# Two-layer NSA/MoBA decoder with experts: gathers and gate transposes moved in the expert pairs, half of layer 1's output projection in three fp32r products

## What is computed

```python
def reference(x, ...):
    for layer in range(2):
        mix = nsa_mixer(x, ...) if layer == 0 else moba_mixer(x, moba_w_in, moba_w_out)
        x = layer_norm(DN_ALPHA * x + mix, ...)
        x = layer_norm(DN_ALPHA * x + grouped_moe(x, ...), ...)
    return x

def moba_mixer(h, w_in, w_out):        # 256 tokens are one block: causal attention, 16 heads of 64
    q, k, v = split(h @ w_in, 3)       # w_in 1024 x 3072, rotary on q and k
    o = softmax(causal(q k^T / 8)) v
    return o @ w_out                   # the output projection, 1024 x 1024

def grouped_moe(h, router_w, router_bias, w_gate, w_up, w_down):   # 16 experts, 2 chosen per token
    gate = ...                         # 256 x 16, two nonzero in a row
    for e in range(16):
        he = silu(h @ w_gate[e]) * (h @ w_up[e])       # 1024 x 512 each
        out = out + (he @ w_down[e]) * gate[:, e:e+1]  # 512 x 1024
```

## Time and profile before

| | us |
|---|---|
| median of three runs | 739.78 (739.68 to 740.61) |
| the profiled execution, its own time | 741.22 |
| its span, from first to last instruction | 739.4 |
| expert matmuls begin, layer 0 / layer 1 | 172 / 522 |
| PE busy in the span | 721.2 (98%) |

### The profile page before, as it was taken

One profiled execution on the slowest core, in us unless ns is written; L12 is line 12 of the kernel. 1 busy time (PEld: TensorE's weight loads), 2 busy tenths in 40 slices (PEclk: granted clock), 3 DMA queues, 4 the chain that ended last, 5 costly groups with the idle time before them and its releaser, 6 DMA issues.

```text
span 739.4 us, 9052 instructions
## 1 busy us (share of the span) xinstructions
PE 721.2 (98%) x3696; PEld 391.8 (53%) x3696; DVE 281.5 (38%) x528; ACT 204.0 (28%) x467; POOL 110.1 (15%) x91
## 2 busy tenths in 40 slices
PE   9999999999999999999999999999999999999994
PEld 5877766774344344343368886646434434434331
DVE  4485675363212121121257785526322212112114
ACT  4443689332101110110033555714111011011001
POOL 0011378322000000000052221401200000000001
PEclk9999999999999999999999999999999999999998
DMA  9999900167999999999999964017799999999992
GB/s 329 304 368 418 405 3 1 58 233 297 423 425 429 430 425 429 426 425 422 413 388 387 414 267 187 6 57 285 271 425 428 425 428 428 428 425 429 419 412 84
DMA packets 45596, 245.06 MB, mean 331 GB/s; under 512 B 6256, under 2 KB 10480, under 8 KB 31728
## 3 DMA queue, kind: packets, MB, share of 16 engines
q1 hardware_dynamic: 45552, 244.43, 82.0%
HBM read 243.37 MB, written 1.05 MB: 331 GB/s over the span
## 4 chain that ended last, share of the span: by engine, by line
PE 88%; DVE 6%; ACT 2%; POOL 1%; issue 1%; DMA 1%; SPq 0%; DVEq 0%; ACTq 0%
PE ps L963 30%; PE ps L986 15%; PE ps L883 5%; PE ps L996 4%; PE ps L630 4%; PE ps L632 3%; PE ps L631 3%; PE ps L948 3%; PE ps L776 2%; PE ps L762 2%; PE ps L801 2%; ACT R L1273 1%; PE ps L974 1%; PE ps L939 1%; DVE R L1591 1%
## 5 line engine op out<-in xcount | busy, mean ns | idle before, releaser
L963 PE MATMUL ps<-ring,R 128*64 128x512 f32 x928 | 226.7, 595 | 0.0
L963 PEld LDWEIGHTS ps<-ring,R 128*64 128x64 f32 x928 | 70.3, 137 | 108.8 <-issue 107.2
L986 PE MATMUL ps<-ring,R 128*64 128x512 f32 x448 | 113.4, 595 | 0.8 <-issue 0.8
L1224 ACT ACTIVATE wh<-ps,small 128x512 fp32r<-128x512 f32 x32 | 22.0, 687 | 262.3 <-PE ps L986 260.5
L986 PEld LDWEIGHTS ps<-ring,R 128*64 128x64 f32 x448 | 35.8, 137 | 67.1 <-issue 64.8
L1578 DVE TENSOR_TENSOR wl_r<-ring,wh 128x512 fp32r<-128x512 f32 x72 | 55.4, 787 | 39.7 <-ACT wh L1202 39.3
L1804 DVE SCALAR_TENSOR_TENSOR wl_r<-ps,small,wh 128x512 fp32r<-128x512 f32 x32 | 24.0, 751 | 105.5 <-ACT wh L1224 104.7
L630 PE MATMUL ps<-wh,xh_r 128*128 128x512 f32 x144 | 57.7, 400 | 1.1 <-DVE wl_r L1578 1.0
L1202 ACT CAST wh<-ring 128x512 fp32r<-128x512 f32 x72 | 44.5, 623 | 47.3 <-PE ps L632 45.3
L632 PE MATMUL ps<-wh,xl 128*128 128x512 f32 x144 | 56.3, 391 | 0.0
L631 PE MATMUL ps<-wl_r,xh_r 128*128 128x512 f32 x144 | 56.1, 390 | 0.0
(11 more groups left out here) (237 smaller groups left out, 998.4 us busy)
## 6 DMA issues: line engine op xcount, KB each, us to landing
ring<-in_w_gate SPq DMA_DIRECT2D x24, 2048.0 KB, 17.5
ring<-in_w_up SPq DMA_DIRECT2D x18, 2048.0 KB, 18.7
ring<-in_w_down SPq DMA_DIRECT2D x18, 2048.0 KB, 19.2
ring<-in_w_in SPq DMA_DIRECT2D x20, 1024.0 KB, 14.4
ring<-in_w_gate SPq DMA_DIRECT2D x16, 1024.0 KB, 15.5
ring<-in_w_down SPq DMA_DIRECT2D x24, 512.0 KB, 20.1
ring<-in_w_up SPq DMA_DIRECT2D x12, 1024.0 KB, 11.5
ring<-in_w_out SPq DMA_DIRECT2D x8, 1024.0 KB, 14.9
```

The source lines that it names most:

```text
L963: last = mm(ps[64 * e:64 * e + 64, to, :], xe[:, j, at + 64 * e:at + 64 * e + 64], slots[e][:, j * UNIT:(j + 1) * UNIT], start=(j == 0), s ...
L986: last = mm(ps[64 * e:64 * e + 64, 2 + w, :], hT[:, k, 64 * e:64 * e + 64], slots[e][:, at:at + UNIT], start=(k == 0), stop=(k == FJ - 1))
```

## The change

1. In the expert pairs that gather (0 to 5): the transposes of the gate values move from between gate and up to behind the transposes of the hidden rows, and the second gather moves ahead of down and into bank 0. DVE's `slot_tables` and ACT's copy of gathered rows move accordingly.
2. Half a chunk of each expert phase, the first half of chunk 11 (`ROOM`), goes to a free place in R5, `room`, and is loaded right behind chunk 8.
3. In layer 1 the first four of eight blocks of the output projection become three fp32r products. ACT rounds the eight weight blocks (two units, four blocks) inside its loop over units 8 to 12, behind block 4 and block 7 of each (`out_weights_hi`), into the slot of unit 7; POOL subtracts behind the rotary adds. The attention output's first two groups are rounded by ACT (`group_hi`, behind the exponentials of items 5 and 7) and their rest is made by DVE in `collect`.
4. Unit 7's slot is busy longer, so the slots turn by one: only five chunks are loaded ahead of the end of layer 1's output projection, and chunk 7 comes in two halves.

```diff
-        PIECED = 6
+        PIECED = [6, 4]
...
+                if what == ("moe", 6 * PAIRS):
+                    line.append(line.pop(0))
...
+        ROOM = SLOT + 3
+        room = R5[:, 0:2 * D]
...
-            elif n in U0:
-                l = U0.index(n)
-                eng.wait_ge(L.proj, base[l].proj + T)
+            elif n == U0[0]:
+                eng.wait_ge(L.proj, base[0].proj + T)
+            elif n == U0[1]:
+                eng.wait_ge(L.mix, base[1].mix + 2 * T)
...
+            def load_first_of_split():
+                sp.wait_ge(L.mix, base[1].mix + T + 1)
+                load_part_of_split(0)
...
+            def load_room(n):
+                l = n // (6 * PAIRS)
+                sp.wait_ge(N.x_ready, ready(2 * l, T - 1, 1))
+                i, k = divmod(n % (6 * PAIRS), 6)
+                sp.dma_start(room, expert_src(l, 2 * i + k % 2, k // 2)[:, 0:2 * D]).then_inc(landing(("moe", n), 0)[0], 16)
...
-                ahead = SLOT - 2
+                ahead = SLOT - 2 - l
...
-                        if w and i % 2 and more:
-                            pe.wait_ge(rd.xa, 2 * g + 3)
+                        if i % 2 and more:
+                            pe.wait_ge((rd.xa, rd.xe)[w], 2 * g + 3)
+                        elif i and i % 2 == 0 and w == 0:
+                            pe.wait_ge(rd.xa, 2 * g + 2)
...
-                        if w == 0:
-                            pe.wait_ge(rd.gp, g + 1)
-                            if i:
-                                pe.wait_ge(rd.y_lo, 2 * n)
-                            transpose_gates(rd, 2 * (i % 2))
+                        if w == 0 and not more:
+                            gates_of_pair()
...
                     transpose_hidden(rd)
+                    if more:
+                        gates_of_pair()
...
                     pe.wait_ge(rd.ht_sb, n + 1)
+                    if more:
+                        gather(rd, 0, (2 * part + 2, 2 * part + 3), 4 * SLOTS)
                     pe.wait_ge(rd.gsum, n + 1)
...
-                    if more:
-                        pe.wait_ge(rd.xe, 2 * g + 2 + i % 2 + 1)
-                        gather(rd, 1, (2 * part + 2, 2 * part + 3), 4 * SLOTS)
...
+                def group_hi(u):
+                    act.wait_ge(L.pv, B.pv + ITEMS[l] // 4 * (u + 1))
+                    copy(OT2_HI[u], ps[:, 6 + u % 2, :]).then_inc(L.ot_sb, 1)
+
+                def out_weights_hi(n):
+                    w, j = WO[1][n]
+                    if n == 0:
+                        act.wait_ge(L.proj, base[1].proj + T)
+                    act.wait_ge(*landing(("unit", OUT[2 + w]), j // 4))
+                    copy(wo_hi_at(1, w, j), in_slot(("unit", OUT[2 + w]))[:, j * UNIT:(j + 1) * UNIT]).then_inc(wo_hi, 1)
...
                             split_hi(7 + i, j)
+                            if i < 5 and j in (4, 7):
+                                out_weights_hi(2 * (i - 1) + j // 7)
...
                     exponentials(m)
+                    if l and m in (5, 7):
+                        group_hi(m // 2 - 2)
...
+                    if l and r:
+                        out_weights_lo(r - 1, *WO[1][r - 1])
+                    if l and r == 7:
+                        out_weights_lo(7, *WO[1][7])
...
-                if l == 0 and u < 3:
+                if u < PIECED[l] // 2:
                     dve.wait_ge(L.ot_sb, B.ot_sb + 2 * u + 1)
                     tt(OT2_LO[u], ps[:, bank, :], OT2_HI[u], ALU.subtract).then_inc(L.ot_sb, 1)
```

More of the change, by code:

```diff
@@ L1 @@
 from collections import namedtuple
+from functools import partial
 from contextlib import ExitStack
@@ L314, in in_slot, with chunks_at @@
             return ring[:, n] if n < SLOT else extra
+        ROOM = SLOT + 3
+        room = R5[:, 0:2 * D]
+        def chunks_at(what, j):
+            if what[0] == "moe" and what[1] % (6 * PAIRS) == ROOM and j < KJ // 2:
+                return room[:, j * UNIT:(j + 1) * UNIT]
+            return in_slot(what)[:, j * UNIT:(j + 1) * UNIT]
+        spare_slots = [lambda j, n=n: ring[:, n, j * UNIT:(j + 1) * UNIT] for n in range(6)]
         def landing(what, h):
@@ L475, in load_half_freed @@
                             slot_free(what)
+                        if h == 0 and what[1] % (6 * PAIRS) == ROOM:
+                            continue
                         i, k = divmod(what[1] % (6 * PAIRS), 6)
@@ L557, in _ @@
                 for n in range(ahead, SLOT + 1):
+                    if ("moe", 6 * PAIRS * l + n) == SPLIT_FREED:
+                        load_rest_of_split()
+                        continue
                     load_expert(6 * PAIRS * l + n)
+                    if n == ahead and l:
+                        load_first_of_split()
+                load_room(6 * PAIRS * l + ROOM)
                 load_quarters(6 * PAIRS * l + SLOT + 1)
@@ L1008, in experts, with gates_of_pair @@
                     chunks = [("moe", 6 * n + k) for k in range(6)]
[L1009 removed]
+                    slots = [partial(chunks_at, c) for c in chunks]
                     more = i // 2 + 1 < DUOS
                     part = 2 * (i % 2)
+                    def gates_of_pair():
+                        pe.wait_ge(rd.gp, g + 1)
+                        if i:
+                            pe.wait_ge(rd.y_lo, 2 * n)
+                        transpose_gates(rd, 2 * (i % 2))
                     for w, done in ((0, rd.gate_done), (1, rd.up_done)):
@@ L1237, in experts @@
                     silu(rd)
+                    if i // 2 + 1 < DUOS:
+                        part = 2 * (i % 2) + 1
+                        act.wait_ge(rd.gathered, 4 * g + 4 + part + 1)
+                        copy_rows(rd, XeT[(i // 2 + 1) % 2], 0, range(2 * part, 2 * part + 2), 4 * SLOTS)
                     act.wait_ge(rd.gsum, n + 1)
@@ L1820, in experts @@
                         most = dve.value_load(over[0:1, 0:1], min_val=0, max_val=S)
-                    dve.wait_ge(rd.gt, n + 1)
-                    slot_tables(rd, i % 2)
+                    if not more:
+                        dve.wait_ge(rd.gt, n + 1)
+                        slot_tables(rd, i % 2)
                     dve.wait_ge(rd.silu, n + 1)
```

65 lines of the change are left out of this document (37 added, 28 removed).

## The result

The changed kernel took **766.78 us** (760.85 to 766.95, three runs) where the kernel before took 739.78: a ratio of 1.033, 95% interval 1.029 to 1.036. The profiled execution took 766.78, its span is 764.9 instead of 739.4. So it is slower, as forecast, but by 27 us and not by 11; 766.8 lies outside the range of 744 to 756.

What follows compares the result with a forecast made beforehand. PE's own sequence bounds the expert pairs, DMA close behind. Terms +7.1 +2.1 +1.2 +5.7 -2.2 -3.1 = +10.8 on the median 739.8 gave 750.6 us, range 744 to 756 (8 in 10).

Steps and rivals of the forecast that it cites:

- half clock behind one wait: Unit 8: after PE's idle time the clock stays at the lower level for a stretch, costing 2.1 us (0 to 3.4).
- Part 1: Expert pairs: the new order saves 0.51 us per gathering pair (0.35 to 0.65), 3.1 us per layer.
- Everything behind lands 2.5 us earlier, so 1.0 us of room is left: Expert pairs' DMA: the half chunk fills a hole, later chunks land 2.5 us earlier, and the gain stands in full.
- Part 2, the landing: Unit 8: ACT's cast waits for unit 13's first half, landing at 407.6; PE starts block 5 7.1 us later.
- the rival in which the weights do not hold ACT up: Unit 13's half there in time, keeping layer 0's gain: 738.3 us; needs landing 9 us earlier than 407.6; chance 0.05.
- the stretch 733 to 734: Profile row cited for the clock falling when PE rests: PE idle, granted 0.82, on its way from 1.00 to half.
- Part 2, contention: Layer 1's projection units: POOL's eight subtractions slow DVE at eight more meetings, most hidden: 1.2 us (0 to 6).
- The rival that I gave that rule: "Heavier": VectorE and POOL exclude each other wholly, +10.2 instead of 1.2, 759.6 us; chance 0.08.
- Part 3: Layer 1's attention: DVE's subtractions wait for ACT's casts behind the exponentials, delaying PE twice, 5.7 us net (0 to 7).
- Part 4: Output projection: three products replace a float32 block, 0.18 us less each, twelve behind the loop: 2.2 us saved.

Runs made afterwards that it cites:

- run 8: Only the change's expert-pair part (layer 1's output projection as before), without the half chunk's own place, its bytes loaded behind the quarters again: 738.09 us.
- Run 5: Changed kernel with ACT's eight output-weight casts one unit later (units 9 to 12), POOL's subtractions two rotary adds later: 753.40 us.
- run 9: Changed kernel with casts one unit later, subtractions on DVE, both attention moves, PE's layer 1 jump kept: 743.76 us; without the jump 734.99; expert-pair part alone 736.24.
- run 6: Changed kernel, layer 1 attention: ACT's group cast ahead of the item's exponentials, DVE's subtraction behind the next item's copy: 759.10 us, profiled execution 753.19.
- run 4: Changed kernel with POOL's eight output-weight subtractions all behind layer 1's last rotary add instead of one behind each: 765.50 us.

## Why the forecast was right in sign and wrong in size

Four terms of the sum failed. It had none for the layout of PE's program (7.4 us in the trace), 1.2 for contention where 4.9 came, half clock behind one wait where it came behind three (2.6 missing), and it let DMA keep up where PE waited 1.2 in layer 1.

**Part 1, right, except DMA.** Gate to up took 6.87 (forecast 6.92), the pair 0.63 less instead of 0.51, inside 0.35 to 0.65. The failing step is "Everything behind lands 2.5 us earlier, so 1.0 us of room is left": the landing came 1.6 earlier. Up to 215.77 the chunks behind `room` landed 2.5 or more earlier; 0.9 was lost at the next chunk, with DMA at its full rate, and run 8 leaves open by what. PE gained 4.2, had 1.6 of old room and 1.6 of new, and waited 1.1 in each layer. In layer 0 it did not matter, in layer 1 it cost 1.2.

**Part 2, the landing: right.** Forecast 407.6, measured 408.54, 0.9 late like the chunks of part 1; PE at 409.6, measured 410.53; idle 10.2, measured 10.9; half clock 2.1, measured 2.4. Run 5 takes it away and gets 12.7 back at once, 13.3 in the end. One condition was miscounted: the rival in which the weights do not hold ACT up needs the landing 10.2 us earlier, by as much as PE idles, and not 9. And the stretch 733 to 734, which I called a second, is a microsecond.

**Part 2, contention: the mechanism was named, its size was off.** The forecast took 1.2 of 0 to 6; it was 4.9. I argued from one meeting before, in which DVE lost 0.75 and PE nothing, that most of eight would be hidden. Two things were missed. First, the new subtraction follows POOL's rotary add without a gap, so that the meeting lasts 3.4 us and not 1.66, longer than DVE's lead of one block. Second, it took 1.74 and not 1.27. DVE's own durations show how it goes. These are DVE's two subtractions behind 447.27 in the trace of after, least, middle and longest in ns, beside POOL's add from 446.56 to 448.23 and its subtraction from 448.19 to 449.93:

```profile
L1655 DVE TENSOR_TENSOR wl_r<-ring,wh x2: 1509/1643/1777, 447.3 to 448.7; 128x512 fp32r<-128x512 f32 x2
```

The first ends at 447.27 + 1.51 = 448.78, 0.55 behind the end of POOL's add; the second at 448.70 + 1.78 = 450.48, 0.55 behind the end of POOL's subtraction. Each stood until POOL's instruction was over and then did its work. By the rule of the Trainium skill, "SBUF - State Buffer", section "SBUF: two separate sides", this is what happens to a VectorE instruction with two SBUF inputs beside a GpSimd one that reads SBUF: the shared port is held for a whole instruction. The trace agrees. The rival that I gave that rule (759.6, chance 0.08) had the right mechanism, though a part of it was hidden: 4.9 instead of 10.2. Of the 4.9, 3.2 lie ahead of 454.4. The other 1.7 lie at 454 to 458, where two small operations of DVE (the router's folded weights) took 1.3 us each beside POOL's last two subtractions, 0.3 each in the kernel before, and PE waited 1.4.

**Part 3, right in its waits, wrong in what follows them.** Waits forecast 3.4 and 2.3 more net, measured 3.3 and 2.5. But I charged the clock only at unit 8. Behind both waits it was granted 0.67 and 0.64 for four microseconds:

```profile
488.00:492.00 4.00, 4.00 (x32) 2.79 (x28) 0.75 (x2) 1.88 (x10) 1.69 (x1) 0.67 0.00 0
...
498.00:502.00 4.00, 4.00 (x26) 3.15 (x22) 1.02 (x2) 0.37 (x1) 1.55 (x1) 0.64 0.02 4
```

That is 2.6 us that my own working of unit 8 should have given: here a wait of 3 us has the same tail as one of 11, only shorter. It is not sure to come: the first of the two waits has it in four of the five traces in which it stands, and in run 5 not.

**Part 4** was forecast at 0.18 a block; between 514.81 and 517.64 four blocks of three products take 2.83, and four float32 blocks behind them 518.08 to 521.51, 3.43: 0.15 a block.

**What the forecast left out: the layout of PE's program,** 5.7 + 1.7 us in the trace and 9 by run 9. The line with `pe.addr_align` in `experts` is not touched by the change, and I passed over it. Its effect depends on how many instructions stand ahead of it, and the change added 30. I had read which instructions the change moves, not where in the program they lie. With this term, 3.7 more of contention, 2.6 of clock and 1.2 of DMA, the sum of 10.8 becomes 25.7; the traces differ by 25.5. The small errors that are left cancel: 1.0 and 0.3 more at unit 8 and 0.3 more in the output projection stand against the 1.6 that the execution shown of before lost at the router, and that is luck.

The chances were right about the sign, and none of the rivals had several heavy terms at once. All four errors have one sign: three were costs that I took as hidden or as nothing, and the fourth I had not seen.

What stays open is what decides whether the block's packet gets through under full load (the profiled execution of run 6) or waits for the end of the weights (eight of twelve executions of run 9). Where the packets of both queue up, the profile doesn't tell.

## What to carry to other kernels

When an engine's program is strictly in order, ask for each new wait when the awaited thing lands and what is queued behind; this arithmetic held to 1 us here, and moving the wait by one unit took the whole cost away. Charge a wait of PE of 3 us or more with a tail at half clock (1.1 to 2.4 us here), and give a POOL instruction that joins another without a gap the length of both. After a change that adds instructions, count where jumps and aligned places now lie in the compiled program: in the traces here the aligned jump was free 248 and 250 instructions behind a block's start, and 9 or 24 behind it, with the weights' queue full, it cost 5 to 6 us in six of seven.

## What the runs showed of the hardware that was not expected

- PE's instruction blocks come over the DMA engines that carry the weights. With weights at about 400 GB/s, a jump 9 or 24 instructions behind a block's start cost 5.2 to 6.2 us of standing and then a stretch at half clock, and PE went on 2.6 to 2.7 us behind the start of the 16 KB packet. The same jump took 0.3 to 0.4 us where the block was there. The Trainium skill, "Runtime: NRT & Kernel Launch", section "Instruction fetch mechanics", has the sequencer fetch the next page while it runs the current one, calls the cost of a boundary mostly hidden, and warns of jumps out of the two pages. The first agrees: in layer 1's pairs packets ran at 603.0, 627.4, 652.2 and 677.9, about one per pair, and PE waited for none. The second holds here only while the fetch has time: the jump went to the very next page, and still stood.
- DVE's fp32r subtraction waits out a whole instruction of POOL that reads SBUF: 1.51 and 1.78 us instead of 0.69.
- POOL's 128x512 subtraction took 1.74 us in layer 1's projections, 12.78 / 8 = 1.60 with eight in a row behind them (run 4), and 1.27 in layer 0's attention. I had priced it by the row from another stage.
